# Attaching one semaphore wait of a TensorE matmul to the matmul itself

## The reference, cut to what matters

```
for i in range(DEPTH):                      # DEPTH = 2
    mod = (silu(c) @ ada_w[i] + ada_b[i]).reshape(B, 6, 1024)
    h = modulate(rms_norm(x, norm1_g[i]), mod[:, 0], mod[:, 1])
    out = chunk_gmlp_mixer(h, ...) if i == 0 else mamba2_mixer(h, ...)
    x = x + mod[:, 2] * out
    h = modulate(rms_norm(x, norm2_g[i]), mod[:, 3], mod[:, 4])
    x = x + mod[:, 5] * (square(relu(h @ mlp_w1[i])) @ mlp_w2[i])
y = rms_norm(x, final_g)
```

## Time and profile before

| what | value |
|---|---|
| median of 2 runs | 4314.84 us (4313.25 to 4316.44) |
| profiled execution, its own time | 4281.57 us |
| its span on the slowest core (core 1) | 4279.8 us |
| spans of the 8 cores | 4247.6 to 4279.8 us |
| mean granted TensorE clock, by core | 0.807 to 0.811 |
| busy: TensorE matmul / VectorE / ScalarE / GpSimd | 69% / 37% / 23% / 18% of the span |

### The profile page before, as it was taken

One profiled execution on the slowest core, in us unless ns is written; L12 is line 12 of the kernel. 1 busy time (PEld: TensorE's weight loads), 2 busy tenths in 40 slices (PEclk: granted clock), 3 DMA queues, 4 the chain that ended last, 5 costly groups with the idle time before them and its releaser, 6 DMA issues.

```text
span 4279.8 us, 49661 instructions; the slowest of 8 cores (4247.6 to 4279.8 us)
## 1 busy us (share of the span) xinstructions
PE 2957.7 (69%) x17582; PEld 1746.9 (41%) x17582; DVE 1588.7 (37%) x3951; ACT 986.3 (23%) x1882; POOL 779.6 (18%) x1083
## 2 busy tenths in 40 slices
PE   5353644385869799585979968597996758665346
PEld 2121211163634346373434547343454634364224
DVE  0130200045542334554243355424326543345544
ACT  0020200032321322232133223223323222122211
POOL 0010000024420201432010153301105340012010
PEclk9676877696979899797979978698998869786557
DMA  9889989960413344041434414143341403484434
GB/s 239 165 126 154 148 168 138 188 222 4 158 50 128 133 133 168 20 158 40 138 120 135 160 39 158 40 138 136 130 158 60 158 20 132 153 301 141 133 118 151
DMA packets 107262, 562.68 MB, mean 131 GB/s; under 512 B 8990, under 2 KB 42014, under 8 KB 51375
## 3 DMA queue, kind: packets, MB, share of 16 engines
q1 hardware_dynamic: 96914, 466.91, 32.2%
q0 software_dynamic: 10112, 92.59, 14.7%
HBM read 592.71 MB, written 92.59 MB: 160 GB/s over the span
## 4 chain that ended last, share of the span: by engine, by line
PE 55%; DVE 11%; DMA 10%; POOL 8%; ACT 7%; another core or an unknown queue 6%; issue 3%; SPq 0%; DVEq 0%; POOLq 0%; ACTq 0%
PE bank L698 11%; PE bank L680 10%; PE bank L849 5%; PE bank L390 4%; PE bank L1156 3%; PE bank L835 3%; PE bank L657 3%; PE bank L885 3%; DMA sb_wslot<-wsc 3%; PE bank L624 3%; DMA sb_wslot<-w_ada 2%; PE bank L582 2%; POOL sb_arena L1102 2%; PE bank L1053 2%
## 5 line engine op out<-in xcount | busy, mean ns | idle before, releaser
L680 PE MATMUL bank<-sb_h_fm,sb_wslot 128*128 128x512 bf16 (+1 forms) x2560 | 516.5, 363 | 91.6 <-DMA sb_wslot<-wsc 41.1
L698 PE MATMUL bank<-sb_arena,sb_wslot 128*128 128x512 bf16 (+1 forms) x2560 | 478.6, 349 | 55.9 <-DMA sb_wslot<-wsc 50.8
L854 POOL TENSOR_SCALAR sb_arena<-sb_identb,sb_pfmt 128x128 bf16<-128x128 bf16 x576 | 214.8, 373 | 1166.8 <-ACT sb_h_fm L494 725.7
L680 PEld LDWEIGHTS bank<-sb_h_fm,sb_wslot 128*128 128x128 bf16 x2560 | 238.3, 101 | 368.6 <-issue 144.3
L698 PEld LDWEIGHTS bank<-sb_arena,sb_wslot 128*128 128x128 bf16 x2560 | 230.1, 98 | 303.0 <-issue 64.1
L515 DVE SCALAR_TENSOR_TENSOR sb_x_fm<-bank,sb_modT,sb_x_fm 128x512 f32<-128x512 f32 (+1 forms) x160 | 103.0, 644 | 669.4 <-PE bank L698 440.4
L687 DVE SCALAR_TENSOR_TENSOR sb_arena<-bank,sb_arena 128x512 bf16<-128x512 f32 (+1 forms) x320 | 195.7, 611 | 347.0 <-ACT sb_arena L684 286.6
L849 PE MATMUL bank<-sb_h_fm,sb_wslot 128*128 128x256 bf16 (+1 forms) x2304 | 283.3, 267 | 0.0
L390 PE MATMUL bank<-sb_wslot,sb_cT 128*17 128x256 f32 x768 | 180.0, 399 | 128.7 <-DMA sb_wslot<-w_ada 128.7
L684 ACT ACTIVATE sb_arena<-bank 128x512 f32<-128x512 f32 (+1 forms) x320 | 170.6, 533 | 373.6 <-PE bank L680 369.8
L466 ACT ACTIVATE sb_arena<-sb_x_fm 128x512 bf16<-128x512 f32 (+1 forms) x200 | 93.8, 551 | 660.7 <-PE bank L698 381.8
(11 more groups left out here) (186 smaller groups left out, 4206.5 us busy)
## 6 DMA issues: line engine op xcount, KB each, us to landing
sb_wslot<-wsc SPq DMA_DIRECT2D x364, 1024.0 KB, 5.5
wsc<-w_all POOLq DMA_DIRECT2D x30, 2048.0 KB, 83.2
sb_wslot<-w_ada SPq DMA_DIRECT2D x48, 1024.0 KB, 11.4
sb_arena<-xin SPq DMA_DIRECT2D x17, 512.0 KB, 4.4
y_out<-sb_arena POOLq DMA_DIRECT2D x17, 512.0 KB, 2.9
sb_Rt<-sst SPq DMA_DIRECT2D x16, 512.0 KB, 4.1
sb_x_fm<-sst SPq DMA_DIRECT2D x16, 512.0 KB, 4.2
ssm_s<-sb_Rt POOLq DMA_DIRECT2D x16, 512.0 KB, 5.0
```

The source lines that it names most:

```text
L680: kb.op("pe", lambda kc=kc, sv=sv, mi=mi, bk=bk: nc.tensor.matmul(banks[bk][:, 0:T], lhsT=sv[:, mi, kc, :], rhs=h_fm[:, kc, 0:T], start=(k ...
L698: kb.op("pe", lambda kc=kc, sv=sv, bk=bk: nc.tensor.matmul(banks[bk][:, 0:T], lhsT=sv[:, kc, :], rhs=hid[:, kc, 0:T], start=(kc == 0), sto ...
L854: kb.op("pool", lambda k=k, j=j, jb=jb: nc.gpsimd.tensor_scalar(out=dg[:, jb, k, :], in0=identb[:], scalar1=pfm[:, PF_CW + k * 32 + j:PF_C ...
```

## The change

`_deps` and `op` get an argument `lhs`, the resources of the stationary operand. For TensorE, if `lhs` is given, the list `todo` is searched from its end for a wait that is not needed for `lhs` beyond what this engine has already waited for. The first such wait is taken out of the list and attached to the matmul; all others stay separate wait instructions ahead of it. At most one wait is attached to one matmul.

```diff
-    def _deps(self, eng, reads, writes):
+    def _deps(self, eng, reads, writes, lhs=None):
...
         if todo and eng != "pe":
             attach = todo.pop()
+        elif todo and lhs is not None:
+            lneed = {}
+            for r in lhs:
+                if r.w is not None:
+                    k, v = r.w
+                    if lneed.get(k, 0) < v:
+                        lneed[k] = v
+            for i in range(len(todo) - 1, -1, -1):
+                k, v = todo[i]
+                if lneed.get(k, 0) <= self.seen[eng].get(k, 0):
+                    attach = todo.pop(i)
+                    break
         for k, v in todo:
             self._wait(eng, k, v)
```

```diff
@@ mlp, first product
-                            start=(kc == 0), stop=(kc == KC - 1)), reads=[sr, R_h[kc]], writes=[bres[bk]])
+                            start=(kc == 0), stop=(kc == KC - 1)), reads=[sr, R_h[kc]], writes=[bres[bk]], lhs=[sr])
@@ scan, step B2b
-                                  reads=[R_ysq[yb], R_ones], writes=[bres[3]])
+                                  reads=[R_ysq[yb], R_ones], writes=[bres[3]], lhs=[R_ones])
@@ scan, step A
-                          reads=[R_mc], writes=[bres[sbk]])
+                          reads=[R_mc], writes=[bres[sbk]], lhs=[R_mc])
...
-                                                         start=False, stop=True), reads=[R_cst, R_rda[rb]], writes=[bres[sbk]])
+                                                         start=False, stop=True), reads=[R_cst, R_rda[rb]], writes=[bres[sbk]], lhs=[R_cst])
```

More of the change, by code:

```diff
@@ L126, in _attach, with op @@
             self.seen[eng][k] = v
-    def op(self, eng, fn, reads=(), writes=()):
+    def op(self, eng, fn, reads=(), writes=(), lhs=None):
         if self.dry:
             return
-        attach = self._deps(eng, reads, writes)
+        attach = self._deps(eng, reads, writes, lhs)
         ins = fn()
@@ L471, in rms_rstd @@
                                                          start=(i == 0), stop=(i == n - 1)),
-                      reads=[R_sq[i], R_ones], writes=[bres[bk]])
+                      reads=[R_sq[i], R_ones], writes=[bres[bk]], lhs=[R_ones])
             kb.op("act", lambda: nc.scalar.activation(out=banks[bk][:, 0:T], in_=banks[bk][:, 0:T], func=AF.Ln,
@@ L583, in gmlp @@
                             banks[bk][:, :], lhsT=h_fm[:, kc, ti * 128:(ti + 1) * 128], rhs=sv[:, kc, :],
-                            start=(kc == 0), stop=(kc == KC - 1)), reads=[sr, R_h[kc]], writes=[bres[bk]])
+                            start=(kc == 0), stop=(kc == KC - 1)), reads=[sr, R_h[kc]], writes=[bres[bk]], lhs=[R_h[kc]])
                     kb.op("act", lambda nb=nb, bk=bk, zb=zb: nc.scalar.activation(
@@ L634, in gmlp @@
                             rhs=wstb[:, g * 128:(g + 1) * 128], start=True, stop=True),
-                            reads=[R_n[ti], R_wstb], writes=[bres[bk2]])
+                            reads=[R_n[ti], R_wstb], writes=[bres[bk2]], lhs=[R_n[ti]])
                     sb_ = ssb[:, ub, :].rearrange("p (a b) -> p a b", b=128) if False else None
@@ L658, in gmlp @@
                             banks[bk][:, 0:T], lhsT=sv[:, mi, kc, :], rhs=us_fm[:, kc, 0:T],
-                            start=(kc == 0), stop=(kc == 15)), reads=[sr, R_us16[kc]], writes=[bres[bk]])
+                            start=(kc == 0), stop=(kc == 15)), reads=[sr, R_us16[kc]], writes=[bres[bk]], lhs=[sr])
                     resid_add(T, c, bk, l, 0, sample, tmp, tmpR)
@@ L699, in mlp @@
                         banks[bk][:, 0:T], lhsT=sv[:, kc, :], rhs=hid[:, kc, 0:T], start=(kc == 0), stop=(kc == 31)),
-                        reads=[sr, R_hid[kc]], writes=[bres[bk]])
+                        reads=[sr, R_hid[kc]], writes=[bres[bk]], lhs=[sr])
                 resid_add(T, c, bk, l, 1, sample, tmp, R_tmp)
@@ L887, in conv_emit @@
                                 rhs=(xpre_s[:, jb, :, k:k + LS] if sample else xpre[:, jb, k:k + T]), start=(k == 0), stop=(k == 3)),
-                                reads=[R_dgp[jb], R_dgv[jb], R_xp[jb]], writes=[bres[b2]])
+                                reads=[R_dgp[jb], R_dgv[jb], R_xp[jb]], writes=[bres[b2]], lhs=[R_dgp[jb], R_dgv[jb]])
                         if j < 16:
@@ L1031, in mamba @@
                                                              lhsT=BC[:, g, cc], rhs=BC[:, 8 + g, cc], start=True, stop=True),
-                          reads=[R_bc[g], R_bc[8 + g]], writes=[bres[4 + g // 4]])
+                          reads=[R_bc[g], R_bc[8 + g]], writes=[bres[4 + g // 4]], lhs=[R_bc[g]])
                 def stSTD(_):
@@ L1071, in stB1 @@
                             rhs=xdt[:, h * HD:(h + 1) * HD], start=True, stop=True),
-                            reads=[R_M[mb], R_xdt], writes=[bres[0]])
+                            reads=[R_M[mb], R_xdt], writes=[bres[0]], lhs=[R_M[mb]])
                     if sample:
@@ L1081, in stB1 @@
                                                                             rhs=STb[:, g * 256:(g + 1) * 256], start=True, stop=True),
-                                  reads=[R_bc[8 + g], R_STb], writes=[bres[1]])
+                                  reads=[R_bc[8 + g], R_STb], writes=[bres[1]], lhs=[R_bc[8 + g]])
                         kb.op("dve", lambda: nc.vector.tensor_tensor(
@@ L1142, in mamba @@
                                                                  rhs=xdtd[:, g * 256:(g + 1) * 256], start=True, stop=True),
-                              reads=[R_btm, R_xdtd], writes=[bres[g // 2]])
+                              reads=[R_btm, R_xdtd], writes=[bres[g // 2]], lhs=[R_btm])
                     for q in range(4):
@@ L1157, in mamba @@
                             banks[bk][:, 0:T], lhsT=sv[:, mi, kc, :], rhs=yg[:, kc, 0:T], start=(kc == 0), stop=(kc == 15)),
-                            reads=[sr, R_yg[kc]], writes=[bres[bk]])
+                            reads=[sr, R_yg[kc]], writes=[bres[bk]], lhs=[sr])
                     resid_add(T, c, bk, l, 0, sample, ntmp, [R_nt0, R_nt1], c0=c0)
```

1 line of the change is left out of this document (removed).

## The result

| | kernel before | kernel changed |
|---|---|---|
| median of all executions | 4397.02 us (13) | 4267.09 us (14) |
| profiled execution | 4281.57 us | 4258.63 us |
| span on its slowest core | 4279.8 us | 4256.8 us |
| median span of its cores, die 0 / die 1 | 4261.0 / 4262.3 us | 4247.1 / 4242.8 us |
| ratio, after / before | | 0.9912, 95% interval 0.9879 to 0.9945 |

A forecast was written before the change was run, and what follows sets the result against it. TensorE's matmuls were taken as 55% of the span, with separate waits costing only where TensorE idles. Scan 11.6 + norms 4.4 + late weights 0.9 = 17 us, taken from the median 4314.84 us: 4298 us (-0.4%), range 4262 to 4325.

The forecast's parts named there:

- What bounds, and what costs nothing: TensorE holds 55% of the chain; satisfied waits run under earlier matmuls in dense stretches and cost the array nothing.
- slower rival: Attached waits cost up to one weight load, 0.098 us, at 1200 dense output tiles: 4416 us (+2.3%); chance 6%.
- much faster one: Separate waits cost the array more than read; 0.11 us at 1200 tiles, another 132 us: 4166 us (-3.4%); chance 3%.
- The load going ahead: At idle places with only one wait, attaching it lets the weight load run ahead, saving 0.14 - 0.03 = 0.11 us.
- signs named for it: At L470 the last matmul starts 0.03 to 0.05 us after ScalarE's square, its load standing before the square's end.
- third rival: Saved tenths are taken up elsewhere, or the wait gates the weight load; median stays 4315 us; chance 12%.
- The sum of places: Idle places in scan, norms and late weights at 0.11 us each: 11.6 + 4.4 + 0.9 = 17 us; elsewhere nothing.
- 153 places: Places counted as gaining 0.11 us each: 105 in the scan, 40 in the norms, 8 weight stalls.
- scan: TensorE idle 105 times before L1112, L1053, L1140 and L1050, 0.11 us each: 11.6 us.
- norms: Only each norm's last wait counts: 25 at L470, 15 at L680 and L835, 0.11 us each: 4.4 us.
- all the rest: Outside scan and norms only 8 late-weight stalls at L698 were counted, 0.9 us; elsewhere nothing.
- weight stalls: Weights landing late, 8 stalls at L698: the bank's wait after the slot's goes, 0.9 us; the stalls themselves stay.

The follow-up runs named there:

- run 11: Kernel before with each of TensorE's 3725 separate waits issued twice: 4339.0 us in the one undisturbed execution, ratio 1.0140.
- run 2: Changed kernel with `lhs` left only at seven matmuls of the scan, against the kernel before: 4281.3 us, 12 us less; ratio 0.9995.
- run 3: Changed kernel with `lhs` left only at the norms' matmuls (L482, L594, L692, L847), against the kernel before: 4285.0 us, 8 us less; ratio 0.9993.
- run 5: Changed kernel with `lhs` left only at seven matmuls outside scan and norms: 4284.5 us against 4292.4 for the kernel before, ratio 0.9974.
- run 1: Changed kernel again, no edit, beside the kernel before: undisturbed median 4268.7 us against 4293.1, ratio 0.9937.
- run 4: Changed kernel with the wait list searched from the front, so the operands' wait is attached: 4258.3 us, 35 us less than the kernel before.
- run 7: Every TensorE instruction with a wait gets the first of its list attached: 4262.1 us, 30 us less than the kernel before, ratio 0.9911.

## Why the prediction was wrong

**What bounds, and what costs nothing: right.** The satisfied waits under the dense matmuls cost nothing before, nothing when they are gone, and nothing when they are doubled (run 11). The slower rival (0.098 us for each of 1200 tiles) is out by the same rows: L710 has its 55.42 us with the waits attached. So is the much faster one.

**The load going ahead: wrong.** The prediction had 0.14 - 0.03 us for a place with a single wait "and the load now goes ahead". The rows of the norm show the load itself released by the wait. The signs named for it failed with it: the load does not stand before the end of the square, and the matmul starts 0.06 us after it, not 0.03 to 0.05. The place gives 0.14 - 0.06 = 0.08 us. The part of the third rival that says so, "the wait really gates the weight load", is what happened; its price, nothing, was not. One of several waits gives 0.10 us (0.33 to 0.23), as forecast.

**The sum of places: wrong, and this is the step that failed.** "Elsewhere it is nothing, covered by the matmul in flight" was read from two dense prompt stretches and applied to everything outside the 153 places. Against the terms, by undisturbed medians of executions and by all cores of undisturbed dies:

| term | forecast | executions | cores |
|---|---|---|---|
| scan (run 2) | 11.6 us | 12 us | 9.9 us |
| norms (run 3) | 4.4 us | 8 us | 3.4 us |
| all the rest (run 5) | 0.9 us | 8 us | 7.5 us |
| together (run 1) | 17 us | 24 us | 23 us |

The rest is the mis-sized term. Part of what it lacks can be read in the prediction itself: at L1112, where the late wait stays separate and the bank's is attached, it counted 0.11 us; at L885 it found that the late operand's wait "stays separate" and counted nothing, though there too TensorE stood idle (31 times) with the bank's wait in the list. The convolution is 1.9 us shorter by the start-to-start sum. The remaining 6 us of run 5 I cannot place. The forecast's 0.9 us for the weight stalls is not shown by any run: at L710 the sum is 2.3 and 0.2 us shorter in the two traces of the changed kernel, and 2.4 shorter in run 2, where nothing is attached there.

The scan's 11.6 us is right in part by luck. Its four lines measure 4.8 (L1112), 2.5 (L1053), 1.1 (L1140) and 3.3 us (L1050), where 5.7, 2.3, 1.8 and 1.8 were forecast. L958, L1030 and L1069, which the prediction did not count, are 1.2, 0.7 and 0.6 us shorter, and some of it comes back at L938 (1.5 us longer) and L926 (0.6).

**The comparison: of the 38 us (0.0088 x 4298) some 14 are, as far as run 1 tells, not the change.** 4298.2 is the mean of the six counted executions of before, of which three stood at 4313 to 4316; run 1, where the kernel before had none of the kind but one (4309.6), gave 0.9937. This is the greater part of the distance from 17 to 38 us, and no step of the mechanism. The prediction was built on a median of two executions that both stood there. It noted the 33 us between them and the profiled one, and used them as width, not as a level.

**Third rival, nothing: wrong**, but it has a share. Run 4's gain at L1124 comes back in part before L1062, and the 540 waits of run 7 brought nothing that shows.

What remains open: where 6 of the rest's 8 us lie, if it is 8 (run 5's interval begins at 3); whether the 4313 us executions of the first comparison were those of a lower clock; and whether a wait on the matmul alone, with its load ahead of it, would give the last 0.05 us, which was not tried.

## What to carry to other kernels

Count a separate wait only where its engine is idle when the last semaphore arrives, and then count every instruction between that semaphore and the work: putting the late wait last, with none attached, was worth nearly as much here as attaching one (20 and 24 us). An idle place with a late wait that stays separate still gains if another wait of its list goes. When a list of waits has one that is attached, attach the one that will be late, not the last one written. And before a gain below 1% is forecast against a median of two executions, look at whether the executions of both kernels had the same granted clock.

## What the runs showed of the hardware

- A wait attached to a matmul is carried by its weight load: all 1885 in the changed kernel's trace. After GpSimd or ScalarE, the load starts 0.05 us behind the producer's end; behind one separate wait it is 0.11 to 0.12 us, and each further wait adds 0.10 to 0.12.
- The separate waits of a whole stretch can be doubled without a longer stretch, even with matmuls of 0.109 us. So far as these rows go, a satisfied wait is executed under the matmuls in flight. Where TensorE is idle they cost: 18.6 us more at step B2b with its waits doubled.
- With the wait on the load the matmul is recorded 0.00 to 0.01 us behind the load's start, where it stood 0.03 us behind it after a separate wait.
